# Block attention: key pages turned by VectorE, a unit's scores by 16 small tiles

## What is computed

```
k_past = k_pool[page_table].reshape(db, PAST_LEN, KV_HEADS, HEAD_DIM)
kb = k_past[:, :own_start].reshape(db, nbf, MOBA_BLOCK, KV_HEADS, HEAD_DIM).transpose(0, 3, 1, 2, 4)
kmean = jnp.mean(kb.astype(jnp.float32), axis=3)
gate = jnp.einsum('bkgsd,bknd->bkgsn', qg.astype(jnp.float32), kmean)
gval, gidx = lax.top_k(gate, ksel)
k_sel = kb[bi, ki, gidx]
bias_sel = jnp.where(ok[..., None], -slope[..., None] * dist_sel, NEG_INF)
o = _moba_attend(qg, k_own, v_own, bias_own, k_sel, v_sel, bias_sel)
```

## Time and profile before

| what | value |
|---|---|
| median of 3 runs | 2062.57 us (2061.17 to 2063.12) |
| profiled execution | 2062.47 us |
| its span, first to last instruction | 2060.8 us |
| granted TensorE clock, mean | 0.991 of full |
| PE busy | 2007.0 us (97%) |
| VectorE, ScalarE, POOL busy | 1162.9, 937.8, 209.0 us |
| read and written in HBM | 349.48 and 21.19 MB |

### The profile page before, as it was taken

One profiled execution on the slowest core, in us unless ns is written; L12 is line 12 of the kernel. 1 busy time (PEld: TensorE's weight loads), 2 busy tenths in 40 slices (PEclk: granted clock), 3 DMA queues, 4 the chain that ended last, 5 costly groups with the idle time before them and its releaser, 6 DMA issues. The chain is left out here.

```text
span 2060.8 us, 40011 instructions
## 1 busy us (share of the span) xinstructions
PE 2007.0 (97%) x15754; PEld 1913.0 (93%) x15754; DVE 1162.9 (56%) x1844; ACT 937.8 (46%) x1533; POOL 209.0 (10%) x362
## 2 busy tenths in 40 slices
PE   6999999999999999999999999899999999999996
PEld 6899999999999999999999999899888888999996
DVE  5647766657465564556544544744554555555446
ACT  7435455425344253344433335534555555443443
POOL 1001000010110101000000000020234333200000
PEclk9999999999999999999999999999999999999998
DMA  9386555465564656755555566496788888765741
GB/s 249 113 237 182 143 144 144 131 184 142 164 169 133 185 139 169 210 148 143 149 148 145 154 181 216 123 279 182 217 262 269 256 252 248 233 183 158 246 152 64
DMA packets 539532, 373.27 MB, mean 181 GB/s; under 512 B 14907, under 2 KB 509688, under 8 KB 538474
## 3 DMA queue, kind: packets, MB, share of 16 engines
q1 hardware_dynamic: 519666, 306.53, 52.7%
q0 software_dynamic: 19680, 64.20, 9.7%
HBM read 349.48 MB, written 21.19 MB: 180 GB/s over the span
## 5 line engine op out<-in xcount | busy, mean ns | idle before, releaser
L123 ACT ACTIVATE w_high<-w_raw 128x2048 fp32r<-128x2048 f32 x232 | 443.7, 1912 | 625.5 <-PE bank L172 553.6
L128 DVE TENSOR_TENSOR w_low<-w_raw,w_high 128x2048 fp32r<-128x2048 f32 x232 | 530.8, 2289 | 218.2 <-ACT w_high L123 218.1
L167 PE MATMUL bank<-x_hi,w_high 128*128 128x320 f32 x1664 | 494.2, 312 | 0.0
L167 PE MATMUL bank<-x_lo,w_high 128*128 128x320 f32 x1664 | 489.6, 309 | 0.0
L167 PEld LDWEIGHTS bank<-x_hi,w_high 128*128 128x128 f32 x1664 | 312.3, 188 | 1.0
L167 PEld LDWEIGHTS bank<-x_lo,w_high 128*128 128x128 f32 x1664 | 312.5, 188 | 0.6
L172 PE MATMUL bank<-x_hi,w_low 128*128 128x320 f32 x1664 | 260.9, 309 | 0.0
L172 PEld LDWEIGHTS bank<-x_hi,w_low 128*128 128x128 f32 x1664 | 248.3, 188 | 0.0
L167 PE MATMUL bank<-xo_x_hi,w_high 128*128 128x320 f32 x640 | 198.0, 323 | 1.9 <-issue 1.6
L167 PE MATMUL bank<-xo_x_lo,w_high 128*128 128x320 f32 x640 | 188.9, 309 | 0.0
L2227 POOL DMA_DIRECT2D value_pages<-in_cache_v x232 | 124.9, 538 | 212.9 <-issue 134.7
(11 more groups left out here) (453 smaller groups left out, 3457.5 us busy)
## 6 DMA issues: line engine op xcount, KB each, us to landing
w_raw<-in_ev_w_in SPq DMA_DIRECT2D x104, 1024.0 KB, 5.7
w_raw<-in_od_w_in SPq DMA_DIRECT2D x40, 1024.0 KB, 6.7
w_raw<-in_ev_w_out SPq DMA_DIRECT2D x32, 1024.0 KB, 5.8
key_pages<-in_cache_k SPq DMA_DIRECT2D x256, 128.0 KB, 3.0
value_pages<-in_cache_v POOLq DMA_DIRECT2D x232, 128.0 KB, 3.4
w_raw<-in_ca_w_kv SPq DMA_DIRECT2D x16, 1024.0 KB, 7.2
w_raw<-in_ca_w_q SPq DMA_DIRECT2D x16, 1024.0 KB, 5.9
w_raw<-in_od_w_out SPq DMA_DIRECT2D x16, 1024.0 KB, 5.8
```

Source lines behind the costliest of these rows:

```text
L123: self.nc.scalar.activation(self.w_high[n % HI][:], self.w_raw[n % RAW][:], ACT.Copy).then_inc(self.w_hi, 1)
L128: self.nc.vector.tensor_tensor(self.w_low[n % RAW][:], self.w_raw[n % RAW][:], self.w_high[n % HI][:].bitcast(F32), ALU.subtract).then_inc ...
L167: e.nc.tensor.matmul(out, hi[:, k, cols], rhs(k)[part], start=(k == 0 and part == 0), stop=False)
```

## The change

- `HI` goes from 3 to 2, `AHEAD` from 2 to 1. In `Moba`, `high` moves from a tile's last quarter to its first, `low` from the second quarter of the next tile to the third of its own.
- `Opening`: the memory norm's weights get a DMA of their own, issued by ScalarE; PE waits for that one, and turns the other small loads after kv tile 0. The dt projection is 16 matmuls in plain 32-bit floats on the unsplit input, in four column groups, with weights that VectorE scales by the norm's; twelve small matmuls add the groups. Chunks of x are turned up to one tile earlier.
- Keys: two places of a whole unit (`keys_of`, one for each sequence), eight chunks; all issued by SP, from the unit before's scores on. VectorE turns each chunk in place in 32x32 blocks (`flip`, one instruction over 128x1024). K is gone, and with it `past_keys`.
- X: PE spreads the queries by 16 matmuls so that each row group of 32 holds each block of 32 dimensions; ScalarE copies the result to `qx`.
- S: once a unit, 64 matmuls, tiles of 32 rows by 32 columns over 512 keys, into banks 2 to 5 (three of them also take turns). ScalarE copies all four to `ms_p` ("raw"); VectorE's four `scored` read that, two a quarter.
- A unit comes every 13 quarters, not 12: S at 3, T at 9 + 2a (16 + 3a before), V at 11 + 2a (19 + 3a), `unit_out` at 19 (30), OT at 20 (31).

```diff
@@ -30,7 +30,7 @@
...
-RAW, HI, AHEAD = 4, 3, 2
+RAW, HI, AHEAD = 4, 2, 1
...
@@ -394,9 +399,8 @@
     def tensor(self, pe):
         e, s, f, nc = self.e, self.s, self.f, self.e.nc
         pe.wait_ge(s["consts_in"], 16)
-        pe.wait_ge(s["rows_in"], 16 * 8)
-        for i in self.vec:
-            f.tensor(pe, i)
+        pe.wait_ge(s["memw_in"], 16)
+        f.tensor(pe, self.memw)
...
-        pe.wait_ge(s["dtw_lo"], 2)
+        pe.wait_ge(s["dtw"], 2)
         pe.wait_ge(s["var"], 2)
         for k in range(KC):
-            pe.wait_ge(s["x_lo"], k + 1)
-            for n, (p, q) in enumerate(((0, 0), (0, 1), (1, 0))):
-                m = nc.tensor.matmul(e.bank[7][0:SSD_HEADS, 0:T], self.wdts[p][:, k, :], e.a_rhs(k)[q],
-                                     start=n == 0 and k == 0, stop=n == 2 and k == KC - 1)
+            f.out_of(pe, self.x[k])
+            c = 32 * (k % 4)
+            m = nc.tensor.matmul(e.bank[7][c:c + 32, 0:T], self.wdts[:, k, :], e.xt[:, k, :], start=k < 4, stop=k >= KC - 4, skip_group_check=True)
...
@@ -2099,29 +2099,29 @@
...
-    BASE0, PERIOD = 40, 12
-    SC, TN, MI, PR = 2, (3, 4, 5), 6, 7
-    TAIL, CHUNKS, SHARED = 14, 5, 26
+            "turned", "turn_out", "flipped", "scores", "raw", "own_scores", "biased", "own_biased", "biases", "exped", "recips", "v_used", "o_ready", "o_rows",
+            "p_scores", "p_biased", "p_max", "p_exped", "p_recip", "p_probs", "g_hi", "g_lo", "gs_gated", "swish"]
+    BASE0, PERIOD, SCORE = 40, 13, 3
+    SC, TN, MI, PR = (2, 3, 4, 5), (3, 4, 5), 6, 7
+    TAIL = 14
...
-        self.kring = [e.at(f"key_pages{i}", 144 + 4 * i, [128, 4, 256]) for i in range(4)]
-        self.kt_past = e.at("past_keys", 160, [128, 4, 512])
+        self.keys_of = [e.at(f"key_pages{i}", kb, [128, NPG, 256]) for i, kb in enumerate((144, 76))]
...
+        self.vring = [e.at(f"value_pages{i}", kb, [128, 4, 256]) for i, kb in enumerate((92, 96, 160, 164))]
...
-        self.pp = [e.at(f"ms_p{i}", 4 + 2 * i, [128, 512]) for i in range(self.CHUNKS)]
+        self.pp = e.at("ms_p", 4, [128, NPG, PAGE])
+        self.qx = e.at("ms_q_by_block", 12, [128, 4, 128])
...
-        for U in self.rel(qr, 31):
+        for U in self.rel(qr, 20):
             yield "OT", U, 0
         for a in range(4):
-            for U in self.rel(qr, 19 + 3 * a):
+            for U in self.rel(qr, 11 + 2 * a):
                 yield "V", U, a
                 if a == 3:
...
         for a in range(4):
-            for U in self.rel(qr, 16 + 3 * a):
+            for U in self.rel(qr, 9 + 2 * a):
...
-        for a in range(4):
-            for U in self.rel(qr, 2 + 3 * a):
-                yield "S", U, a
-                if a == 3:
-                    yield "S", U, 4
-            for U in self.rel(qr, 3 * a):
-                yield "K", 4 * U + a, 0
-                yield "K", 4 * U + a, 1
+        for U in self.rel(qr, self.SCORE - 1):
+            yield "X", U, 0
...
+        for U in self.rel(qr, self.SCORE):
+            yield "S", U, 0
...
+    def loads(self, qr):
+
+        if qr % 2 == 0:
+            for i in range(8):
+                if qr == 14 + 2 * i:
+                    yield 0, i
+        for U in range(1, 8):
+            for i in range(8):
+                if qr == self.BASE0 + self.PERIOD * (U - 1) + self.SCORE + 1 + max(0, i - 1):
+                    yield U, i
+
+    def flips(self, qr):
+
+        for i in range(8):
+            if qr == self.BASE0 - 16 + 2 * i:
+                yield i
+        for U in range(1, 8):
+            for i in range(8):
+                if qr == self.BASE0 + self.PERIOD * U + self.SCORE - 8 + i:
+                    yield 8 * U + i
+
+    def key_tile(self, c):
+
+        return self.keys_of[c % 2][:, 4 * (c // 2 % 4):4 * (c // 2 % 4) + 4, :]
+
+    def flip(self, dve, c):
+
+        dve.wait_ge(self.k_in[c % 8], 64 * (c // 8 + 1))
+        x = self.key_tile(c).rearrange("p g c -> p (g c)")
+        self.e.nc.vector.transpose(x, x).then_inc(self.s["flipped"], 1)
...
         for qr in range(4 * len(self.order)):
             if qr % 4 == 0 and qr:
                 e.load(sp, m + qr // 4 - 1 + RAW)
-            for Q in range(2):
-                if qr == 22 + 8 * Q:
-                    for bi in range(2):
-                        self.page(sp, "k", Q, bi, None)
-            for Q in range(30):
-                if qr == self.BASE0 + 3 * Q + 1:
-                    for bi in range(2):
-                        self.page(sp, "k", Q + 2, bi, (s["turned"], self.fill[("K", Q, bi), 1] + 1))
-            for Q in range(self.SHARED, 32):
-                if qr == self.BASE0 + 3 * Q + 14:
-                    self.page(sp, "v", Q, 1, (s["v_used"], Q - 1))
+            for U, i in self.loads(qr):
+                self.page(sp, "k", 8 * U + i, (s["scores"], U) if U else None)
...
-            for bi in range(2 if Q < self.SHARED else 1):
-                self.page(pool, "v", Q, bi, (s["v_used"], Q - 1) if Q >= 2 else None)
+            for bi in range(2):
+                self.page(pool, "v", 2 * Q + bi, (s["v_used"], Q - 1) if Q >= 2 else None)
...
+        if units:
+            pe.wait_ge(self.s["raw"], units)
...
@@ -2300,42 +2315,43 @@
...
-        if kind == "K":
-            Q, bi = U, a
-            c = 2 * Q + bi
-            pe.wait_ge(*self.landed("k", Q, bi))
-            for hi in range(2):
-                bank = self.turn_bank(pe, step, hi)
-                for g in range(4):
-                    t = nc.tensor.transpose(bank[:, 128 * g:128 * g + 128], self.kring[c % 4][:, g, 128 * hi:128 * hi + 128], e.ident)
-                t.then_inc(s["turned"], 1)
+        if kind == "X":
+            pe.wait_ge(s["q_out"], U + 1)
+            bank = self.turn_bank(pe, step)
+            for db in range(4):
+                for kb in range(4):
+                    t = mm(bank[32 * kb:32 * kb + 32, 128 * db:128 * db + 128], e.ident[:, 32 * db:32 * db + 32],
+                           self.qb[:].rearrange("p b h t -> p (b h t)"), start=True, stop=True)
+            t.then_inc(s["turned"], 1)
         if kind == "S":
-            n = 4 * U + a
-            if a == 0:
-                pe.wait_ge(s["q_out"], U + 1)
-            if a < 4:
-                if n:
-                    pe.wait_ge(s["biased"], n)
-                self.out_of(pe, ("K", n, 1), 1)
-            else:
-                if U:
-                    pe.wait_ge(s["own_biased"], U)
-                if self.heads_by(self.BASE0 + self.PERIOD * U + 11):
-                    pe.wait_ge(s["p_biased"], self.heads_by(self.BASE0 + self.PERIOD * U + 11))
+            pe.wait_ge(s["flipped"], 8 * U + 8)
+            pe.wait_ge(s["turn_out"], self.fills_by[U])
+            if U:
+                pe.wait_ge(s["raw"], U)
+                pe.wait_ge(s["own_biased"], U)
+            for db in range(4):
+                for kb in range(4):
+                    rows = slice(32 * kb, 32 * kb + 32)
+                    for j in range(4):
+                        bi, hi = divmod(j, 2)
+                        c0 = 128 * hi + 32 * db
+                        t = mm(e.bank[self.SC[kb]][32 * j:32 * j + 32, :], self.qx[rows, db, 32 * j:32 * j + 32],
+                               self.keys_of[bi][rows, :, c0:c0 + 32], start=db == 0, stop=db == 3, skip_group_check=True)
+            t.then_inc(s["scores"], 1)
+            heads = self.heads_by(self.BASE0 + self.PERIOD * U + self.SCORE)
+            if heads:
+                pe.wait_ge(s["p_biased"], heads)
             for j in range(4):
                 bi, hi = divmod(j, 2)
                 q = self.qb[:, bi, 4 * hi:4 * hi + 4, :].rearrange("p g t -> p (g t)")
-                if a < 4:
-                    t = mm(e.bank[self.SC][32 * j:32 * j + 32, :], q, self.kt_past[:, j, :], start=True, stop=True)
-                else:
-                    t = mm(e.bank[self.PR][32 * j:32 * j + 32, 128:128 + TSA], q, self.kt[:, 2 * (U // 4) + hi, TP:T], start=True, stop=True)
-            t.then_inc(s["scores" if a < 4 else "own_scores"], 1)
+                t = mm(e.bank[self.PR][32 * j:32 * j + 32, 128:128 + TSA], q, self.kt[:, 2 * (U // 4) + hi, TP:T], start=True, stop=True)
+            t.then_inc(s["own_scores"], 1)
...
@@ -2408,13 +2424,18 @@
...
-        if kind == "K":
-            Q, bi = U, a
-            for hi in range(2):
-                b = bank(hi)
-                if Q and bi == 0 and hi == 0:
-                    act.wait_ge(s["scores"], Q)
-                f(self.kt_past[:, 2 * bi + hi, :], b[:], ACT.Copy).then_inc(s["turn_out"], 1)
+        if kind == "X":
+            b = bank()
+            if U:
+                act.wait_ge(s["scores"], U)
+            f(self.qx[:], b[:].rearrange("p (d c) -> p d c", d=4), ACT.Copy).then_inc(s["turn_out"], 1)
+        if kind == "S":
+            act.wait_ge(s["scores"], U + 1)
+            if U:
+                self.turned(act, ("T", U - 1, 3))
+            for kb in range(4):
```

(43 more changed lines are left out.)

153 lines of the change are left out of this document (74 added, 79 removed).

## The result

The changed kernel takes 2131.05 us, the median of four runs (2126.23 to 2136.8), against 2061.87 for the kernel before beside it: 1.0334 times as long, 95% interval 1.0318 to 1.0349. The forecast was 2056, the range ended at 2084. The profiled execution took 2128.65 us and spans 2127.0, 66.2 more than before.

What follows compares the result with a forecast made beforehand. PE was taken as the bound, busy 2007.0 of 2060.8 us. From 2062.5: opening -9, high weight place +2, matmuls -56, new waits +57 gave 2056.5, so 2056 us; range 2032 to 2084.

Steps and rivals of the forecast that it cites:

- Opening, -9: Start of the kernel: shorter dt projection gives -8 us, first transposes not waiting for small loads -1; range -5 to -13.
- One high place fewer, +2: Weights one slot ahead, not two: 1 us at each of two small cross output projections, 0 to 4.4; 48-matmul tiles nothing.
- Matmuls, -56: Block attention: K and its waits go, 62.0 us; X adds 8, S adds 0, fewer breaks of tile runs add 2.
- the third rival: Block attention: sixteen tiles don't run together; S is 9.8 us, total 2102, or 2152 with column tiles alone; chance 0.10.
- OT, +41: Block attention: PE waits before OT for unit_out behind VectorE's score work, mean 5.8 us, seven units.
- V, +16: Block attention: PE waits some 2 us once a unit before a V for POOL's value load, 12.0 us long.
- The clock, +0: Block attention: the forecast had no term for a lower TensorE clock behind PE's waits.
- The first head's turn, +0: Block attention: the forecast had no term for a wait of PE before the first prompt head's turn.
- The sum of waits: Block attention: new waits of PE before OT and V, +57 us in all, with keys and flips at nothing.
- costing the keys at nothing: Block attention: key loads, flip and S take 44 us a unit, under PE's 46.9, so they add no time.
- The second rival: Block attention: key loads bind at 1.21 us an issue, 50.5 us a unit against 46.9; total 2081; chance 0.20.

Runs made afterwards that it cites:

- opening_alone: Kernel before with the changed opening and two high weight places, its block attention kept but for moved high and low: 2059.23 us, ratio 0.9986.
- opening_three: Kernel before with the changed opening, three high weight places, block attention whole, slot 1 split before the small loads are turned: 2060.13 us.
- short_chain: Changed kernel with VectorE's four score trios behind each S run over 8 of each block's 256 keys: 2088.02 us.
- v_by_act: Changed kernel with the second half of each unit's third pair of value chunks loaded by ScalarE's queue, not POOL's: 2105.25 us.
- shift_half_values: shift_one with each unit's third and fourth pairs of value chunks not loaded, their V steps using the first two again: 2073.88 us.
- ot_late: Changed kernel with only the OT step moved three quarters back, from 20 to 23: 2119.91 us.
- shift_one: ot_late with T, V and the division one quarter later: 2126.44 us.
- short_half: shift_half_values and short_chain in one kernel, against the changed kernel: 2068.26 us, ratio 1.0038 to the kernel before.
- fill_half: Changed kernel with 9 idle matmuls before each OT and each third V, to keep PE at work: 2129.65 us.
- chunked: Kernel before with opening_alone's opening, VectorE key turns and sixteen-tile scores, but S four times a unit at 128 columns: 2110.31 us.

## Why the prediction was wrong

**Opening, -9: the sum right in this execution, in part by luck.** The dt matmuls take 2.3 us for the 2.5 reckoned:

```profile
81.99 2.36 PE L431 MATMUL bank<-xt,w_dt_scaled 128*32 128x320 f32 x32
```

But kv tile 0 of the first projection already starts 4.3 us early (17.16 for 21.45), where the small loads were given 1, and tile 0 of the second ends 12.0 early (91.21 for 103.20), for 9 reckoned. Three of these are gone at the cross attention's first output tile, which no term had. The -9.0 there is the most that any of the twelve traces has; the least is -4.8.

**One high place fewer, +2: about right for the cross attentions (1.3 in all), too small by the block attention.** Its tiles were given nothing; opening_alone loses 2.8 us in them, and with three places and the order of before opening_three loses none.

**Matmuls, -56: right.** Five of the 62 us were waits, so -51 of work, for -50 measured. Sixteen tiles run together: 4.0 us was reckoned for S and 4.4 measured, so the third rival is out. The trace agrees with the Trainium skill's packing (TensorE: Matmul & The Clock Gate, Part 3). A flip is 1.234 us, for which 1.2 was taken:

```profile
L2236 DVE STREAM_TRANSPOSE key_pages<-key_pages 128x1024 f32<-128x1024 f32 x64 | 78.6, 1234 | 32.1 <-DMA key_pages<-in_cache_k 32.1
```

**OT, +41: right, place and price**: seven waits, 43.6 us. The Trainium skill's warning (TensorEngine Tiling (Array Packing), PSUM Bottleneck) is of the copy out of PSUM. The trace agrees only in part: of the 14 us from the scores to OT the copies are 2.07, and 12 are VectorE's work from SBUF.

**V, +16: the term that was mis-sized.** 40.3 us were measured. The step took POOL's eight issues, 8.6 us, and a median landing of 3.4. In the chain above the last of eight issues is out 10.0 us after the V (1597.51 to 1607.54) and its data need 5.70 more (6.11 and 5.56 in two other units), while SP loads keys; the window at 1558 has a DMA share of 1.08. In the last unit, behind which no keys load, the third V starts 3.2 us after the last issue (1831.71 to 1834.91) and waits 3.07, so the key burst is the likely cause; no run takes it alone away. The median over all loads hid the ones that are waited for.

**The clock, +0: the step that failed.** The forecast counted 57 us of new waits and nothing for what a wait does to the matmuls behind it. It is 36 us, half of the miss. The trace before could have shown it: outside the block attention it has six stretches of lower clock, each at a wait of 1.4 to 5.3 us, which by the same sum cost 13.4 us, some 2.2 each. One of them, a wait and the 4 us behind it:

```profile
1213.19 0.60 PE L167 MATMUL bank<-evy_x_hi,w_high 128*128 128x320 f32 x1 [3.83 <-PEq L105]
```

```profile
1213.00:1217.00 4.00, 3.81 (x14) 0.50 1.06 310
```

Sixteen waits at 2.2 would have been 36.

**The first head's turn, +0.** The 8.0 us before it, once, had no term either: VectorE comes to that head only behind the first unit's four trios, its biases and a w_low.

**The sum of waits.** V's 24 more, the clock's 36, the head's 8 and OT's 3 are 71 of the 72 us by which the profiled execution lies above 2056.5. So what failed are the terms above, and with them right the sum of waits comes close for this kernel. It does not say what a repair gains: short_chain, v_by_act and shift_half_values each shorten the chain and gain, but moving a step gains little (ot_late, shift_one), and behind the chain the key loads come close. In the changed kernel no wait ends on a flip, so costing the keys at nothing held there. The second rival's 50.5 us a unit is also what short_half measured for its longest unit, but with an S of 7 us where the rival had 4.0, and its mean is 48.5: the match is partly luck. That rival ended the range, so the range had no case in which its cost and larger waits come together.

Not tried: a second place for a unit's scores, a second key unit, a third pair of value places, or banks for the scores that take no turns. What each would give is open.

No version was found that beats both kernels by more than opening_alone's 0.14%.

## What to carry to other kernels

When a step is batched and its buffers stay single, write down the whole cycle from the batch to the next one, with every load and engine in it, and compare its length with the busiest engine's work; a wait priced alone against that engine tells what it costs now, not what comes back when it is taken away. Price a load that is waited for by its own landing in the burst it falls into, not by the median of all. And where TensorE waits some microseconds at a time, look in the trace at hand for what the clock takes behind such a wait, and add it: here 16 waits of 3 to 9 us cost 36 us more.

## What was not expected of the hardware

A shortened wait drops the clock too: in fill_half idle was cut from 96.0 to 73.5 us and the clock loss only from 37.4 to 30.3, in chunked no wait exceeds 3.3 us and 26 us are lost. Not every wait of that size is followed by the lower clock: in chunked one of 2.1 us is not (the S at 1419.15). An S of sixteen small tiles takes 1.85 us at 128 columns and 4.4 at 512, where a quarter would be 1.1. SP's key issues take 1.0 us each in a unit's first eight and 1.2 in the rest (8.12 for 8, 19.21 for 16, 9.48 for 8); why is open.
